# A two-block transformer forward pass on one core: RMS norms applied behind the projections, last slab of a stage ordered by column halves

## The reference

```python
# first block, one layer (HEAD_DIM 64, D_FF 2816)
n = rms_norm(h, ln_mix_g);  proj = n @ w_in          # attentions, gates
h = h + (gate_a * ya + gate_b * yb) @ w_out
n = rms_norm(h, ln_x_g)
h = h + memory_cross_attn(n, rms_norm(mem, ln_mem_g), w_xq, w_xkv, w_xo)
n = rms_norm(h, ln_ffn_g)
h = h + conv_gated_mlp(n, w_up, conv_w, conv_b, w_down)   # 3-tap conv on 2*2816 channels
x = rms_norm(h, ln_f_g)
# second block, two layers l = 0, 1
h = rms_norm(x, norm1_g[l]);  p = h @ w_in[l]        # pool | gmlp u, v | conv value, gate
x = x + concat([ya, yb, yc]) @ w_out[l]              # yc: 31-tap depthwise conv
h = rms_norm(x, norm2_g[l])
x = x + swiglu(h, ...)   if l == 0 else   x + moe_swiglu(h, router, ...)  # top 2 of 8
return rms_norm(x, final_g)
# rms_norm(x, g) = x * rsqrt(mean(x*x, -1) + 1e-6) * g
```

## Time and profile before

| | |
|---|---|
| median of three executions | 1955.86 us (1954.71 to 1955.98) |
| profiled execution | 1955.43 us |
| its span | 1953.6 us |
| PE busy | 1859.1 us (95%), 10333 matmuls |
| weight loads of PE | 1616.5 us (83%) |
| DVE busy | 1462.9 us (75%) |
| ACT busy | 1171.5 us (60%) |
| GpSimd busy | 52.9 us (3%) |
| mean granted TensorE clock | 0.979 |
| read from memory | 492.88 MB, 253 GB/s over the span |

### The profile page before, as it was taken

One profiled execution on the slowest core, in us unless ns is written; L12 is line 12 of the kernel. 1 busy time (PEld: TensorE's weight loads), 2 busy tenths in 40 slices (PEclk: granted clock), 3 DMA queues, 4 the chain that ended last, 5 costly groups with the idle time before them and its releaser, 6 DMA issues. The chain is left out here.

```text
span 1953.6 us, 25959 instructions
## 1 busy us (share of the span) xinstructions
PE 1859.1 (95%) x10333; PEld 1616.5 (83%) x10333; DVE 1462.9 (75%) x1534; ACT 1171.5 (60%) x1094; POOL 52.9 (3%) x69
## 2 busy tenths in 40 slices
PE   6999988999898999998899999999999999999996
PEld 6988977899797999896788888888888888888884
DVE  6554575776795544695688989989889898998985
ACT  4446745554544343443577767777677776767773
POOL 0000000000320000310000000000000000000000
PEclk9999999999898999999799999999999999999998
DMA  9443444555353655362699999999999999999991
GB/s 302 139 130 129 142 160 136 173 194 193 104 178 98 199 193 177 104 217 108 225 368 356 368 329 366 368 351 366 336 374 354 350 367 340 374 359 346 375 355 43
DMA packets 253853, 495.68 MB, mean 254 GB/s; under 512 B 9537, under 2 KB 95263, under 8 KB 253727
## 3 DMA queue, kind: packets, MB, share of 16 engines
q1 hardware_dynamic: 248927, 488.64, 70.7%
q10 hardware_dynamic: 4800, 5.32, 0.9%
HBM read 492.88 MB, written 1.05 MB: 253 GB/s over the span
## 5 line engine op out<-in xcount | busy, mean ns | idle before, releaser
L351 DVE TENSOR_TENSOR splitL<-raw,splitH 128x2048 fp32r<-128x2048 f32 (+2 forms) x318 | 718.9, 2265 | 260.4 <-ACT splitH L350 255.0
L350 ACT ACTIVATE splitH<-raw 128x2048 fp32r<-128x2048 f32 (+2 forms) x318 | 599.6, 1891 | 167.8 <-PE bank L387 160.7
L385 PE MATMUL bank<-splitH,RBH 128*128 128x512 f32 x1184 | 469.6, 397 | 3.7 <-DVE splitL L351 2.2
L387 PE MATMUL bank<-splitH,RBL 128*128 128x512 f32 x1184 | 462.6, 391 | 0.0
L386 PE MATMUL bank<-splitL,RBH 128*128 128x512 f32 x1184 | 462.4, 391 | 0.0
L385 PE MATMUL bank<-RAH,splitH 128*128 128x256 f32 x1120 | 322.9, 288 | 4.1 <-DVE splitL L351 1.9
L386 PE MATMUL bank<-RAL,splitH 128*128 128x256 f32 x1120 | 319.2, 285 | 0.0
L387 PE MATMUL bank<-RAH,splitL 128*128 128x256 f32 x1120 | 319.0, 285 | 0.0
L351 DVE TENSOR_TENSOR splitL<-rawx,splitH 128x2048 fp32r<-128x2048 f32 x111 | 254.0, 2291 | 35.0 <-ACT splitH L350 33.2
L385 PEld LDWEIGHTS bank<-splitH,RBH 128*128 128x128 f32 x1184 | 223.0, 188 | 51.4 <-issue 4.3
L387 PEld LDWEIGHTS bank<-splitH,RBL 128*128 128x128 f32 x1184 | 222.8, 188 | 47.9
(11 more groups left out here) (275 smaller groups left out, 1791.7 us busy)
## 6 DMA issues: line engine op xcount, KB each, us to landing
raw<-in_moe_wd SPq DMA_DIRECT2D x75, 1024.0 KB, 6.9
raw<-in_moe_wg SPq DMA_DIRECT2D x57, 1024.0 KB, 6.7
raw<-in_moe_wu SPq DMA_DIRECT2D x56, 1024.0 KB, 6.9
rawx<-in_moe_wu SPq DMA_DIRECT2D x38, 1024.0 KB, 7.0
rawx<-in_moe_wg SPq DMA_DIRECT2D x37, 1024.0 KB, 6.7
rawx<-in_moe_wd SPq DMA_DIRECT2D x36, 1024.0 KB, 6.8
raw<-in_w_in SPq DMA_DIRECT2D x29, 1024.0 KB, 5.2
raw<-in_w_up SPq DMA_DIRECT2D x22, 1024.0 KB, 5.5
```

Of the source, the lines that this page charges most:

```text
L350: a = act.op(lambda e: e.activation(h[:, 0:size], r[:, 0:size], ACT.Copy), self.landed[n], over)
L351: d = dve.op(lambda e: e.tensor_tensor(l[:, 0:size], r[:, 0:size], h[:, 0:size].bitcast(F), ALU.subtract), self.landed[n], over, a)
L385: e.matmul(o, lh, rh, start=start, stop=False)
L387: return e.matmul(o, ll, rh, start=False, stop=stop)
```

## The change

All norms but the first two (ln_mix_g, ln_mem_g) and the last are taken apart. The raw rows of X are transposed and split with the gain alone; 1/rms of a token multiplies what the projections give.

- `last_slab` replaces the last `down` and `add_down` of a stage. Its banks come in the order rows 0 left, rows 1 left, rows 0 right; then PE transposes chunks 0 to 3, which need the left halves alone; then rows 1 right. The last slab is taken with the default depth of two.
- `first_pair` multiplies the first up slab of the next stage with chunks 0 to 3 for both units, transposes and splits chunks 4 to 7 (`later`), and multiplies with them. Inside, `rows.finish` computes 1/rms.
- `second_pair` multiplies the second slab's first unit, then spreads 1/rms over all partitions (`spread`: two diagonals, a matmul with ones, a copy into R), then its second unit. Both first slabs are taken with a depth of one.
- `scaled` multiplies a bank by R on DVE. In `ffn` it writes a unit into the tiles `up`, from which ACT and DVE go on; for the mixers' gate it stands before and behind the sigmoid; outputs with tokens on the partitions are scaled by ACT as they leave PSUM, the router's logits by DVE.
- `BothRows` is the double norm between the blocks; the gains of both are multiplied into `gg`.
- The transposes of `wsr` and the copies into `wsT` move behind the "mc" slabs, and the small loads of a stage move from ahead of `ffn` into its third turn (`loads()` at i == 2).

```diff
+        class Rows:
+            def added(self, i, t):
+                tb, h = i // 2, i % 2
+                self.last[i] = act.op(lambda e: e.activation(
+                    scr[:, tb, 512 * h:512 * h + 512], X[:, tb, 512 * h:512 * h + 512], ACT.Square,
+                    accum_out=stat(3 + h, self.slot, tb)), t)
...
+            def last_slab(self, Wt, nH, nL, kcs, *waits, by=None, acc=(0, 1, 2, 3), spare=(4, 5, 6, 7)):
...
+                d0 = add(0, bank(0))
+                self.rows.added(0, d0)
+                d2 = add(2, bank(2))
+                d1 = add(1, bank(1))
+                t = [self.turn(k, spare[k]) for k in range(4)]
+                t3 = bank(3)
+                W.release(Wt[3], t3)
+                for k in range(4):
+                    self.split(k, spare[k], t[k])
+                d3 = add(3, t3)
+                self.rows.added(2, d2)
+                self.rows.added(1, d1)
+                self.rows.added(3, d3)
+
+            def later(self):
+
+                t = [self.turn(4 + k, b) for k, b in enumerate(self.spare)]
+                for k, b in enumerate(self.spare):
+                    self.split(4 + k, b, t[k])
+                self.r, self.tr = self.rows.finish(self.tp)
...
+            def first_pair(self, Wt, bk):
...
+                    wstat(Wt, banks[bk[m]][:, 0:256], nH, nL, m, all8[:4], True, False, ps.free[bk[m]], by=self.n)
+                self.later()
+                tt = [wstat(Wt, banks[bk[m]][:, 0:256], nH, nL, m, all8[4:], False, True, by=self.n)
+                      for m in range(2)]
...
+            def spread(self):
...
+                td = [dve.op(lambda e, tb=tb: e.tensor_scalar(D[:, tb, :], ident, r[:, tb:tb + 1], None, ALU.mult),
+                             self.tr[tb]) for tb in range(2)]
...
+                self.tR = act.op(lambda e: e.activation(R[:, :], banks[b][:, 0:256], ACT.Copy), t)
...
+            def scaled(self, dst, src, *waits):
+
+                return dve.op(lambda e: e.tensor_tensor(dst, src, self.R[:, :], ALU.mult), self.tR, *waits)
...
-                    Wt = W.take("ud", 1 if i == 11 else 2)
+                    Wt = W.take("ud")
...
+                    if i == 0:
+                        bk = [ps.take() for _ in range(4)]
+                        early.append((bk[0:2], lz.first_pair(W.take("ug", 1), bk[0:2])))
+                        early.append((bk[2:4], lz.second_pair(W.take("uv", 1), bk[2:4])))
...
                         for m in range(2):
                             ch = 22 * which + 2 * i + m
-                            src = banks[bk[m]][:, 0:256]
+                            src = up[which][m][:, :]
+                            tq = lz.scaled(src, banks[bk[m]][:, 0:256], tt[m])
+                            ps.free[bk[m]] = [tq]
                             wc = [prm[:, CW + 44 * k + ch:CW + 44 * k + ch + 1] for k in range(3)]
                             ta = act.op(lambda e, D=D, m=m, src=src, wc=wc, ch=ch: e.activation(
                                 D[:, m, :], src, ACT.Identity, bias=pcol("conv_b", ch), scale=wc[2]),
-                                tt[m], gfree[i % 2])
+                                tq, gfree[i % 2])
...
+            def gate_half(u, b, t):
+                t = lz.scaled(sgc[:, u, :], banks[b][:, 0:256], t)
+                ps.free[b] = [t]
+                t = act.op(lambda e: e.activation(sgc[:, u, :], sgc[:, u, :], ACT.Sigmoid), t)
+                tg[u] = lz.scaled(sgc[:, u, :], sgc[:, u, :], t)
```

More of the change, by code:

```diff
@@ L984, in program, with gain @@
+        def gain(name, g0):
+            return lambda k: pcol(name, g0 + k)
         acc_wo = (4, 6, 5, 7)
+        lz = Lazy(gain("ln_x_g", 0), nAH, nAL, Rows(0), ph + 50 * KB)
         for s in range(4):
[L986 to L991 removed]
@@ L1004, in program @@
+        ps.use([4, 5, 6, 7, 0, 1, 2, 3])
+        q_t = {}
+        tt = []
+        bk = [ps.take() for _ in range(4)]
+        tt += lz.first_pair(W.take("xq", 1), bk[0:2])
+        tt += lz.second_pair(W.take("xq", 1), bk[2:4])
+        for u in range(4):
+            q_t[u] = lz.scaled(qB[:, u, :], banks[bk[u]][:, 0:256], tt[u])
+            ps.free[bk[u]] = [q_t[u]]
+        ps.use(range(8))
         st = {}
@@ new lines, in mixers @@
+            bk = [ps.take() for _ in range(4)]
+            tt = lz.first_pair(W.take("mc", 1), bk[0:2]) + lz.second_pair(W.take("mc", 1), bk[2:4])
+            ps.use(range(4, 8))
+            for i, u in enumerate((1, 2)):
+                gate_half(u, bk[i], tt[i])
+            for i, u in enumerate((1, 2)):
+                value_half(u, bk[2 + i], tt[2 + i])
+            some_taps(4)
+            for half in (gate_half, value_half):
+                Wt = W.take("mc")
+                b = ps.take()
+                t = wstat(Wt, banks[b][:, 0:256], nAH, nAL, 0, all8, True, True, ps.free[b], by=ndy)
+                half(0, b, t)
+                W.release(Wt[3], t)
+                some_taps(4)
@@ new lines, in mixers, with f @@
+            b = ps.take()
+            def f(e, b=b):
+                for h in range(4):
+                    last = e.transpose(banks[b][:, h * 128:(h + 1) * 128], wsr[:, h, :], ident)
+                return last
+            t = pe.op(f, ll, ps.free[b])
+            bv = banks[b][:, :].rearrange("p (h i) -> p h i", h=4)
+            tw = [dve.op(lambda e, bv=bv: e.tensor_copy(wsT[0:64, :, :], bv[0:64, :, :]), t),
+                  dve.op(lambda e, bv=bv: e.tensor_copy(wsT[64:128, :, 64:128], bv[64:128, :, 64:128]), t),
+                  dve.op(lambda e: e.memset(wsT[64:128, :, 0:64], 0.0), t)]
@@ L1255, in mixers, with put_r, g @@
+            ps.free[b] = [tw[1]]
+            act.op(lambda e: e.activation(sm[:, 250:251], sm[:, 251:252], ACT.Silu), tg[0], tzero)
+            def put_r(dstf, toks):
+                def g(tb, src, t):
+                    toks.append(act.op(lambda e: e.activation(dstf(tb), src, ACT.Copy, scale=lz.r[:, tb:tb + 1]),
+                                       t, lz.tr[tb]))
+                    return toks[-1]
+                return g
             tv = []
-            for _ in v_proj("mv", 384, put(lambda tb: vn[:, tb, :], tv), nAH, nAL, ndy):
+            for _ in v_proj("mv", 384, put_r(lambda tb: vn[:, tb, :], tv), nAH, nAL, ndy):
@@ L1498, in program @@
                     lr, t_rtH)
-        tx = mixers(1, n6, ll, tx)
+        nxt = Lazy(gain("norm2_g_2", 8), nBH, nBL, Rows(0), ph + 70 * KB)
+        tx = mixers(1, lz, ll, tx, nxt)
+        lz = nxt
         fenced = [q.now() for q in engines]
```

314 lines of the change are left out of this document (192 added, 122 removed).

## The result

The changed kernel takes 1995.24 us (median of 4 runs, 1993.95 to 1996.95) where the kernel before takes 1955.92 beside it: ratio 1.0203, 95% interval 1.0185 to 1.0221. It is slower by 39 us; the prediction was 1991, range 1976 to 2004. The profiled execution took 1993.95 us with a span of 1991.8, 38.5 and 38.2 more than before's.

The account below looks back on a forecast made before the run. PE was taken to set the pace nearly everywhere, but the convolution FFN's ACT/DVE loop had only 0.6 us of slack a turn. Terms summed to +35.2 on 1955.43 us, 1990.6, stated as 1991; range 1976 to 2004.

Parts of the forecast that it names:

- The convolution FFN: From one last slab to the next: products lengthen the ACT/DVE loop to 20.75 us a turn, 239.5 against 197.0 us, +42.5.
- the zero: Start of a stage's last slab, from which the prediction counts all times in a handover.
- Handovers one, four, five and six: Last slab to next stage's first 96 matmuls, or router's first comparison (sixth): -3.0, -6.0, -4.8, -3.6 us.
- The forecast of a second FFN that takes its products for nothing: Second FFN: four products a turn cost nothing, since DVE has 86 of 170 us free.
- Third handover and first mixer: Third handover ends at 32.1 against 30.2 us, +1.9; first mixer's "ma" gets its low half later, +3.4.
- the step "the clock falls as it did": Third handover: PE waits 7.5 us for the diagonals, clock falls as before (mean 0.83), 1.8 us more.
- the third rival: PE's clock falls again: nothing in convolution FFN turns, some 2 us at four or five places elsewhere; 2000 us, chance 0.12.
- Second mixer: Second mixer: "ma" gets its low half 27.6 us after the first pair, since R is ready late; +4.8 us.
- PE's wait in a turn: Convolution FFN: PE idles 3.8 us in each of ten turns, waiting on L351 before each "uv".
- the rival's paragraph: Falling-clock rival's text: a convolution FFN turn of PE needs up to 2 us more, 19, still under 20.75; chance 0.12.
- The first (the stage stays at PE's pace, 1951): Convolution FFN stays at PE's pace if DVE has work during the 0.59 us activation; total 1951 us, chance 0.07.
- The second, handovers without any queueing: Additions and diagonals never stand behind a low half: four handovers 2.6 us shorter, third up to 7.5; 1973 us, chance 0.06.

Follow-up runs that it names:

- products first: Changed kernel with both products of a unit pair in the convolution FFN issued ahead of both activations: 1969.76 us, ratio 1.0069 to the kernel before.
- off the chain: Changed kernel with the 44 convolution FFN products left out and as many unread ones put behind the first pair's sums: 1950.62 us, ratio 0.9971.
- in the gaps: Changed kernel, convolution FFN products kept: first pair's between a turn's two low halves, second pair's behind the first pair's sums: 1954.29 us, ratio 0.9995.
- the SP run: Changed kernel with the seven small loads of the convolution FFN's third turn issued by SP instead of ACT: 1991.69 us, ratio 1.0184.
- the run with one split ahead: Changed kernel with every last slab taken one split ahead instead of two, as before: 1999.56 us, ratio 1.0220.
- the hybrid with four handovers: Changed kernel, products in DVE's gaps, with double norm, norm ahead of the second mixer and mixers' gates as before: 1948.95 us, ratio 0.9963.
- the runs without products: Changed kernel with the convolution FFN's 44 products left out, so the output is another one: 1950.78 us, ratio 0.9977.
- X scaled late: Changed kernel with ACT's scaling of X in the third handover moved behind the mixer's first two gates: 1991.35 us, ratio 1.0180.
- the kernel with only those three: Kernel before with the change at the first, fourth and sixth handover only: 1942.74 us, ratio 0.9930.

## Why the prediction was right, and where it was off

**The convolution FFN, predicted +42.5, measured +42.7.** Every link came out: the pair 4.13 us for 4.14, the wait inside it 0.67 for 0.04 + 0.59 + 0.05, the turn 20.69 for 20.75, the first copy into RBH 28.8 us after the zero for 28.8, the last slab after 239.7 for 239.5. That it is the order and not the amount is shown by three runs (products first, off the chain, in the gaps). The small loads cost 2.1 us for 1.8, the turns 0.06 us less each than forecast, and the two nearly cancel; the SP run shows that it is ACT's time.

**Handovers one, four, five and six.** 21.5, 21.6, 21.6 for 21.7, and 16.7 to the comparison for 16.7. PE waits 1.16 before the first transposes of the first and 1.61 in the others (I had 1.7), and 0.52 to 0.58 in the second half of the slab (0.5). In stages, from one handover to the next: -3.0 for -3.0, -6.0 for -6.0, -3.5 for -3.6. The forecast of a second FFN that takes its products for nothing holds with them.

**Third handover and first mixer, predicted +5.3, measured +7.5.** This is the term of the sum that was mis-sized most. The wait for the diagonals is 7.7 for "7.5", and they come at 27.35 after the zero for 26.9: the gain products and the double chain, 7.2 us in the prediction, take 7.8 (558.52 to 566.29). The pair then ends at 33.2 for 32.1: the step "the clock falls as it did" put too little on the second unit, which runs at the lower level for most of its length (0.53 over the 5.86 us from 571.39 to 577.25, for 5.2 in the prediction). The last slab itself also ran at 0.50 for its first 5.3 us, which the prediction hadn't foreseen; it cost little, since a low half held DVE up to 549.5 and the additions behind it anyway, and the first transposes come 6.8 us after the zero, as forecast (5.75 and 1.0). The stretch to "ma" is then 25.6 for 26.2. What I left out comes behind it. "Ma" itself, after PE's wait of 2.02 us, takes 8.03 us up to the band products (610.86 less 602.83) instead of 6.46 (565.06 less 558.60, the end of the third stretch of the earlier trace rows), at a clock of 0.79. The row of before's band products, and the window of the change:

```profile
565.06 0.66 PE L1287 MATMUL bank<-band,at_rows 128*64 128x256 f32 x4 [0.47 <-ACT at_rows L612]
```
```profile
602.83:610.86 8.03, 7.47 (x48) 7.26 (x48) 8.03 (x12) 1.34 (x3) 0.00 (x0) 0.79 0.74 240
```

1.6 us, in each mixer. That is the third rival, the clock falling again, at one of its places: I had given it 0.12 as a whole, and in this execution it happens at "ma" and in the turns of the convolution FFN, not in the first, second, fourth and fifth handover. The prediction had it depend on how long a wait is. That isn't borne out: behind a wait of 2.02 us at this very "ma" the clock stayed at 1.00 in the run with one split ahead, and it fell behind 1.19 us in the hybrid with four handovers.

**Second mixer:** 27.3 for 27.6 up to "ma", then the same 1.6.

**PE's wait in a turn, predicted 3.8, measured 2.0 to 3.6.** I worked it out as 20.75 less 16.96, at full clock. Where the turn ahead of the wait ran at full clock it is 3.49 us (485.09); where the clock had fallen, the slower matmuls take the rest, and it is 2.0 (402.33). As the rival's paragraph said, a turn of PE then stays under the loop's, and it costs nothing there; but the sign that I gave, a wait of 3.8 before each "uv", was inconsistent with that paragraph.

**The rivals.** The first (the stage stays at PE's pace, 1951) is what the runs without products and with them off the chain look like, 1950.8 and 1950.6; its arithmetic was right and its condition, that DVE has something to do during the activation, wasn't met by the change. The Trainium skill (Perfetto Trace Analysis, Identifying the Most-Contended Engine) takes occupancy as the measure; by the turn's row DVE was at 13.38 of 20.69 us, 65%, and was still half of what set the pace. The second, handovers without any queueing, didn't come: the waits on X and on the diagonals are there, and the run with one split ahead shows that moving the split away from the additions puts it in front of something worse.

```profile
397.35:418.04 20.69, 18.68 (x122) 17.54 (x122) 13.38 (x17) 9.08 (x10) 0.00 (x0) 0.92 0.46 153
```

**The sum.** +35.2 predicted, +38.5 measured between the profiled executions, +38.2 between their spans. Of the 3.0 missing there, 2.2 is the third handover and first mixer, 0.9 the fifth and second mixer, 0.8 the experts, to which the prediction gave no term, and 0.3 the convolution FFN with the sixth handover. Against these stands -1.2 us ahead of the first handover, which is noise: that slab starts at 262.55 in the change, and at 263.90 and 264.04 in the runs with one split ahead and with X scaled late, whose code is the same up to there or nearly so.

**What stays open.** How much of the wait before "ma" is due to the wsT copies, the moved split or the late start of R: only the products' share was tried. Whether POOL, which is idle in the convolution FFN, could do the products: the kernel for it gave no result. And what makes the clock fall behind one wait and not behind another of the same length.

## What to carry to other kernels

Ask of each stage how long its loop through several engines is, not how busy each engine is: here two engines at 70% and 52% had 0.6 us of slack in a turn of 17. An operation put in front of a hand-off to another engine costs its own time and the other engine's; the same operation, placed where its engine waits anyway, cost nothing when its results were not used, and 0.1 us in the length of a turn (3.5 us over the whole run) when they were. So before dropping a change look for a gap to put its work in. A change made at six places has six prices: three places paid 13 us, and the kernel with only those three was the best.

## What the hardware showed that I had not expected

The length of a wait doesn't tell whether the clock falls behind it. After PE waits of 1.16 to 1.61 us in the handovers the granted clock stayed at 1.00 in all four stretches, but behind one of 1.19 us in the hybrid with four handovers it was 0.50 for 5.17 us. Behind waits of 2.0 us in the convolution FFN it was 0.59 for 4.2 us in some turns and 1.00 in others; before "ma" a wait of 2.02 us was followed by 0.79 over 8.03 us in the change and by 1.00 over 6.55 us in the run with one split ahead. Where it fell, it cost PE another 1.5 us, at "ma" (8.03 - 6.55) as in a turn (18.70 - 17.20, from 402.33 and from 464.40 to the next wait), and 1.7 in cross attention.

Four DVE products in a row take 1.41 us where one alone is listed with 0.42: the next starts 0.33 us after the one before, (1.41 - 0.42)/3, so some 0.09 us of each lie under its neighbour. In a chain where each waits for another engine that overlap isn't there, in a block of them it is.
